# Input projections of a gated three-branch block as two by two block products, seven in place of eight

## The reference

```python
h = _rmsnorm_2(x, norm_g[l])
(u_a, v_a, z_a, c_q, c_kv, k_r, z_b, q_c, k_c, v_c, g_c, z_c, gate_logits) = _split_cols(h @ w_in[l])
y_a = _spatial_gating(u_a, v_a, z_a, ...)
y_b = _mla(c_q, c_kv, k_r, z_b, ...)
y_c = _gla(q_c, k_c, v_c, g_c, z_c, ...)
gates = jax.nn.sigmoid(gate_logits + b_gate[l]).reshape(bn, s, N_BRANCH, d)
merged = (gates[:, :, 0] * (y_a @ w_branch[l, 0]) + gates[:, :, 1] * (y_b @ w_branch[l, 1])
          + gates[:, :, 2] * (y_c @ w_branch[l, 2]))
x = x + merged @ w_out[l]
```

## Time and profile before

| | us |
|---|---|
| median of three runs | 2146.69 (2145.61 to 2146.79) |
| the profiled execution | 2143.29 |
| its span | 2141.5 |
| TensorE busy | 2008.7 (94%) |
| VectorE busy | 902.0 (42%) |
| ScalarE busy | 405.2 (19%) |
| mean granted TensorE clock | 0.976 of full speed |

### The profile page before, as it was taken

How to read it: one execution, slowest core, us unless ns; L and a number is a source line. 1 busy time by engine, 2 the same in 40 slices (tenths; PEclk the granted TensorE clock), 3 DMA queues, 4 the chain that set the end, 5 groups by cost and what they waited for, 6 DMA issues and landing times.

```text
span 2141.5 us, 20633 instructions
## 1 busy us (share of the span) xinstructions
PE 2008.7 (94%) x8153; PEld 908.0 (42%) x8153; DVE 902.0 (42%) x1850; ACT 405.2 (19%) x836; POOL 119.8 (6%) x168
## 2 busy tenths in 40 slices
PE   6999987999999999997899888899999999999998
PEld 2445443333333334454333333333445554445553
DVE  1257555544545445674333323224362432362432
ACT  2146311000000003171100000001222221222220
POOL 1001002000000000000100000000100000100000
PEclk9999987999999999998899999999999999999999
DMA  9267446999999995636799999999533333633331
GB/s 357 91 236 260 173 153 227 427 424 427 426 427 427 428 424 229 246 138 226 282 426 425 426 426 425 425 428 368 192 112 118 118 118 130 221 112 118 118 118 59
DMA packets 95042, 584.23 MB, mean 273 GB/s; under 512 B 10044, under 2 KB 12388, under 8 KB 62044
## 3 DMA queue, kind: packets, MB, share of 16 engines
q1 hardware_dynamic: 84400, 559.96, 64.7%
q0 software_dynamic: 10256, 21.86, 3.2%
q10 hardware_dynamic: 288, 1.05, 0.2%
HBM read 589.05 MB, written 4.26 MB: 277 GB/s over the span
## 4 chain that ended last, share of the span: by engine, by line
PE 80%; DMA 11%; DVE 5%; SPq 2%; ACT 1%; issue 1%; DVEq 0%; POOLq 0%
PE bank L740 25%; PE bank L1042 13%; PE bank L745 6%; DMA ring<-in_w_gate 6%; PE bank L899 5%; PE bank L1056 5%; DMA ring<-in_w_up 4%; PE bank L1120 4%; PE bank L1290 3%; PE bank L967 3%; PE bank L690 2%; PE bank L587 2%; PE bank L678 2%; PE bank L728 1%; DMA ring<-in_w_qkv 1%
## 5 line engine op out<-in xcount | busy, mean ns | idle before, releaser
L740 PE MATMUL bank<-ring,big 128*64 128x512 f32 x2464 | 683.9, 601 | 26.8 <-DMA ring<-in_w_gate 10.2
L740 PEld LDWEIGHTS bank<-ring,big 128*64 128x64 f32 x2464 | 217.8, 138 | 387.4 <-issue 374.4
L1042 PE MATMUL bank<-ring,big 128*128 128x512 f32 (+1 forms) x640 | 282.2, 590 | 0.0
L2051 DVE TENSOR_TENSOR big<-bank,big 128x512 f32<-128x512 f32 x192 | 131.6, 685 | 252.6 <-PE bank L745 251.5
L740 PE MATMUL bank<-big 128*64 128x512 f32 x512 | 227.5, 594 | 0.0
L745 PE MATMUL bank<-big 128*128 128x512 f32 x360 | 180.1, 610 | 0.0
L1042 PEld LDWEIGHTS bank<-ring,big 128*128 128x128 f32 x640 | 117.5, 190 | 126.2 <-issue 126.0
L899 PE MATMUL bank<-ring,big 128*128 128x512 f32 x320 | 141.1, 599 | 3.2 <-ACT big L1334 2.0
L1056 PE MATMUL bank<-ring,big 128*128 128x512 f32 x256 | 111.7, 593 | 0.2
L2255 DVE TENSOR_TENSOR big<-big,bank 128x512 f32<-128x512 f32 x32 | 22.0, 688 | 184.3 <-PE bank L740 184.3
L899 PEld LDWEIGHTS bank<-ring,big 128*128 128x128 f32 x320 | 60.7, 192 | 79.2 <-issue 74.2
(11 more groups left out here) (393 smaller groups left out, 2122.5 us busy)
## 6 DMA issues: line engine op xcount, KB each, us to landing
ring<-in_w_gate SPq DMA_DIRECT2D x52, 2048.0 KB, 18.2
ring<-in_w_up SPq DMA_DIRECT2D x51, 2048.0 KB, 21.7
ring<-in_w_down SPq DMA_DIRECT2D x51, 2048.0 KB, 20.8
ring<-in_w_in SPq DMA_DIRECT2D x26, 2048.0 KB, 7.7
ring<-in_w_ada SPq DMA_DIRECT2D x24, 2048.0 KB, 12.7
big<-in_w_up SPq DMA_DIRECT2D x9, 2048.0 KB, 21.5
big<-in_w_down SPq DMA_DIRECT2D x9, 2048.0 KB, 21.8
big<-in_w_gate SPq DMA_DIRECT2D x8, 2048.0 KB, 19.5
```

The costliest lines, as they stand in the source:

```text
L740: ins = nc.tensor.matmul(bank[half * CAP:(half + 1) * CAP, :], lhs[:, k, half * CAP:(half + 1) * CAP], slot_cols(slots[half], k * step + c ...
L1042: ins = nc.tensor.matmul(u[:, 0:cols], HT2[:, k, tile * P:(tile + 1) * P], w[:, 0:KD * cols].rearrange("p (k n) -> p k n", k=KD)[:, k, :], ...
L2051: return r, V.tensor_tensor(r, bank, GATE[tile // LAT][:, half * 512:(half + 1) * 512], ALU.mult)
```

## The change

The input chunks 6 and 7 become equally wide (472 each). They and the three pairs of gate chunks are computed as a product of two by two blocks: the rows are tile 0 and tile 1, the inner halves are the first and last four blocks of `HT2`, the columns the two chunks. Instead of eight block products of four matmuls, seven are formed: `a11b11`, `a12b21`, `s1t1`, `s2t2`, `s3t3`, `s4b22`, `a22t4`. S1 to S4 are sums of rows, made once a layer by VectorE (`mixed_rows`); T1 to T4 are sums of weights, one 128 by 2048 operation each on VectorE (`mixed_weights`), T2 to T4 written in place of a quarter of the weights in the ring. A product that ends another's sum is accumulated in the same bank (`ADDS_TO`), and VectorE reads the bank in between. The fill list has 144 matmuls a layer, and `POINTS` has smaller numbers in the decay chain. The norm scale, and for gates the bias, is applied afterwards (`gate_rows`; the scaling by ScalarE, `s_paired`). Both chunks of a pair stay in the ring until their last block product, and a load goes to the slot that comes free first (`RELEASED`). Three semaphores are dropped, their waits put on others that rise at the same moment.

```diff
+        after = (LAT + 1) * BRANCHES * D
+        T1 = spare[:, after:after + 2048].rearrange("p (k n) -> p k n", k=4)
+        S12 = cut(2048 + 2 * C_GATE, 1024, 2, 512)
+        S34 = spare[:, after + 2048:after + 3072].rearrange("p (s n) -> p s n", s=2)
+        S1, S2, S3, S4 = (v.rearrange("p (k n) -> p k n", k=4) for v in (S12[:, 0, :], S12[:, 1, :], S34[:, 0, :], S34[:, 1, :]))
+        A11, A12 = HT2[:, 0:4, 0:P], HT2[:, 4:8, 0:P]
+        A21, A22 = HT2[:, 0:4, P:2 * P], HT2[:, 4:8, P:2 * P]
...
-        IN_CHUNKS = [(c, min(512, C_GATE - c)) for c in range(0, C_GATE, 512)]
+        LAST_IN = (C_GATE - 6 * 512) // 2
+        IN_CHUNKS = [(c * 512, 512) for c in range(6)] + [(6 * 512 + i * LAST_IN, LAST_IN) for i in range(2)]
         IN_ORDER = (0, 1, 3, 2, 4, 5, 6, 7)
-        BESIDE = [("in", *IN_CHUNKS[i], tile) for i in IN_ORDER[4:] for tile in range(LAT)]
-        BESIDE_IN = len(BESIDE)
-        BESIDE += [("gate", c, 512, tile) for c in range(2 * BRANCHES) for tile in range(LAT)]
-        BESIDE_GATES = len(BESIDE) - BESIDE_IN
+        HALF = KD // 2
+        PAIRED = [(("in", IN_CHUNKS[6][0]), ("in", IN_CHUNKS[7][0]), LAST_IN)]
+        PAIRED += [(("gate", 2 * n), ("gate", 2 * n + 1), 512) for n in range(BRANCHES)]
+        BESIDE = [("unit", i, tile, KD) for i in (4, 5) for tile in range(LAT)] + [("a11b11", 0, None, HALF)]
+        for g in range(len(PAIRED)):
+            BESIDE += [(name, g, None, HALF) for name in ("a12b21", "s1t1", "s2t2", "s4b22", "s3t3")]
+            if g + 1 < len(PAIRED):
+                BESIDE.append(("a11b11", g + 1, None, HALF))
+            BESIDE.append(("a22t4", g, None, HALF))
+        ADDS_TO = {"s4b22": "s1t1", "s3t3": "s2t2", "a22t4": "s3t3"}
+        T_NUMBER = {"s1t1": 1, "s2t2": 2, "s3t3": 3, "a22t4": 4}
+        STEPS = [(m, k) for m in range(len(BESIDE)) for k in range(BESIDE[m][3])]
+        ENDS = [sum(b[3] for b in BESIDE[:m + 1]) for m in range(len(BESIDE))]
...
-                return (n - second_at) % SLOTS2
+                return min((holder[s] if holder[s] < second_at else second_at + RELEASED.index(stream[holder[s]][0]), s)
+                           for s in range(SLOTS2))[1]
...
-        POINTS = {"rows": (18, 20), "heads": (4, 3), "decay": (4, 6), "logs": (9, 10), "exps": (9, 9),
-                  "turned": (4, 4), "states": (6, 5)}
...
+        POINTS = {"rows": (18, 20), "heads": (4, 3), "decay": (3, 6), "logs": (7, 7), "exps": (7, 6),
+                  "turned": (3, 3), "states": (4, 4)}
...
-                    kind, c, cols, tile = BESIDE[m]
-                    w, at_ = weights((kind, layer, c))
-                    u = BANK_F[n % 2]
-                    if k == 0 and n >= 2:
-                        pe.wait_ge(*beside_taken(n - 2))
-                    ins = nc.tensor.matmul(u[:, 0:cols], HT2[:, k, tile * P:(tile + 1) * P],
-                                           w[:, 0:KD * cols].rearrange("p (k n) -> p k n", k=KD)[:, k, :],
-                                           start=(k == 0), stop=(k == KD - 1))
-                    if k == KD - 1:
+                    name, g, tile, ks = BESIDE[m]
+                    u = BANK_F[F_BANK[n]]
+                    if k == 0 and F_BEHIND[n] is not None:
+                        pe.wait_ge(*beside_taken(F_BEHIND[n]))
+                    if name == "unit":
+                        c, cols = IN_CHUNKS[g]
+                        w, at_ = weights(("in", layer, c))
+                        ins = nc.tensor.matmul(u[:, 0:cols], HT2[:, k, tile * P:(tile + 1) * P],
+                                               w[:, 0:KD * cols].rearrange("p (k n) -> p k n", k=KD)[:, k, :],
+                                               start=(k == 0), stop=(k == ks - 1))
+                        last_use[at_] = (s_fin, n + 1)
+                    else:
+                        x, y = (weights((kind, layer, c)) for kind, c in PAIRED[g][0:2])
+                        b11, b12, b21, b22, cols = quarters(layer, g)
+                        if k == 0 and name in T_NUMBER:
+                            pe.wait_ge(s_mix, 4 * (len(PAIRED) * layer + g) + T_NUMBER[name])
+                        a, b = {"a11b11": (A11, b11), "a12b21": (A12, b21), "s1t1": (S1, T1[:, :, 0:cols]), "s2t2": (S2, b11),
+                                "s4b22": (S4, b22), "s3t3": (S3, b12), "a22t4": (A22, b21)}[name]
+                        ins = nc.tensor.matmul(u[:, 0:cols], a[:, k, :], b[:, k, :], start=(k == 0 and name not in ADDS_TO),
+                                               stop=(k == ks - 1), skip_group_check=True)
+                        last_use[x[1]] = last_use[y[1]] = (s_fin, n + 1)
+                        if name == "a22t4":
+                            last_use[y[1]] = (s_fin, beside_index(layer, "s3t3", g) + 1)
+                    if k == ks - 1:
                         ins.then_inc(s_fin, 1)
-                        last_use[at_] = (s_fin, n + 1)
 
             def in_unit(layer, i, tile):
...
-                pe.wait_ge(s_finA, BESIDE_IN * (layer + 1))
+                pe.wait_ge(s_paired, LAT * (layer + 1))
...
+                    if name == "a11b11":
+                        cols = PAIRED[g][2]
+                        act.wait_ge(s_fin, i + 1)
+                        nc.scalar.activation(pair_rows(g)[1][0], BANK_F[F_BANK[i]][:, 0:cols], ACT.Copy).then_inc(s_finA, 1)
+                    if name == "a12b21" and g == 1:
+                        act.wait_ge(*beside_taken(beside_index(layer, "a22t4", 0)))
+                        for tile in range(LAT):
+                            v = PROJ[:, tile, IN_CHUNKS[6][0]:C_GATE]
+                            nc.scalar.activation(v, v, ACT.Copy, scale=rtot[:, tile:tile + 1]).then_inc(s_paired, 1)
...
+                    (z11, z12), (z21, z22) = pair_rows(g)
+                    u = BANK_F[F_BANK[i]][:, 0:cols]
+                    dve.wait_ge(s_fin, i + 1)
+                    if name == "a12b21":
+                        dve.wait_ge(*beside_taken(beside_index(layer, "a11b11", g)))
+                        V.tensor_tensor(z11, u, z21, ALU.add).then_inc(s_finD, 1)
+                        mixed_weights(layer, g, 2)
+                    if name == "s1t1":
+                        V.tensor_tensor(z22, u, z21, ALU.add).then_inc(s_finD, 1)
+                        mixed_weights(layer, g, 3)
+                    if name == "s2t2":
+                        V.tensor_tensor(z12, u, z21, ALU.add).then_inc(s_finD, 1)
+                        mixed_weights(layer, g, 4)
+                    if name == "s4b22":
+                        dve.wait_ge(*beside_taken(beside_index(layer, "s2t2", g)))
+                        V.tensor_tensor(z12, u, z12, ALU.add).then_inc(s_finD, 1)
+                        gate_rows(layer, g - 1, 0)
+                    if name == "s3t3":
+                        V.tensor_tensor(z22, u, z22, ALU.add).then_inc(s_finD, 1)
+                        gate_rows(layer, g - 1, 1)
+                    if name == "a22t4":
+                        V.tensor_tensor(z21, u, z21, ALU.add).then_inc(s_finD, 1)
+                        mixed_weights(layer, g + 1, 1)
+                        if g + 1 == len(PAIRED):
+                            for tile in range(LAT):
+                                gate_rows(layer, g, tile)
+
+            def gate_rows(layer, g, tile):
+
+                if g < 1:
+                    return
+                dve.wait_ge(*beside_taken(beside_index(layer, "a22t4", g)))
+                v = GS[tile][:, (g - 1) * D:g * D]
+                V.scalar_tensor_tensor(v, v, rtot[:, tile:tile + 1], BG[:, (g - 1) * D:g * D], ALU.mult, ALU.add).then_inc(s_gate, 1)
+
+            def mixed_weights(layer, g, which):
+
+                if g == len(PAIRED):
+                    return
+                b11, b12, b21, b22, cols = quarters(layer, g)
+                t1 = T1[:, :, 0:cols]
+                if which == 1:
+                    for kind, c in PAIRED[g][0:2]:
+                        n = at[kind, layer, c]
+                        dve.wait_ge(w_in[slot_of[n]], 16 * arrival[n])
+                    V.tensor_tensor(t1, b12, b11, ALU.subtract).then_inc(s_mix, one(s_mix))
+                dve.wait_ge(s_mix, so_far(s_mix))
+                if which == 2:
+                    V.tensor_tensor(b11, b22, t1, ALU.subtract).then_inc(s_mix, one(s_mix))
+                if which == 3:
+                    V.tensor_tensor(b12, b22, b12, ALU.subtract).then_inc(s_mix, one(s_mix))
+                if which == 4:
+                    V.tensor_tensor(b21, b21, b11, ALU.subtract).then_inc(s_mix, one(s_mix))
+
...
+            def mixed_rows(layer):
+
+                dve.wait_ge(s_outA, marks["rows_turned", layer][0])
+                V.tensor_tensor(S1, A21, A22, ALU.add).then_inc(s_v, one(s_v))
+                dve.wait_ge(s_v, so_far(s_v))
+                V.tensor_tensor(S2, S1, A11, ALU.subtract).then_inc(s_v, one(s_v))
+                V.tensor_tensor(S3, A11, A21, ALU.subtract)
```

(5 more changed lines are left out.)

108 lines of the change are left out of this document (72 added, 36 removed).

## The result

| | before | with the change |
|---|---|---|
| median, us (four runs each, same chip) | 2146.15 (2143.02 to 2146.79) | 2195.35 (2192.17 to 2200.29) |
| the profiled execution | 2143.29 | 2193.02 |
| its span | 2141.5 | 2191.2 |
| mean granted TensorE clock | 0.976 | 0.964 |

The ratio is 1.0234, with a 95% interval of 1.021 to 1.0259. The forecast was 2138.8 us with a range up to 2149, so the sign was wrong and the time lies 46 us above the range.

A forecast was written before the change was run, and what follows sets the result against it. TensorE, busy 94%, was taken to bound the kernel, VectorE being slack. Per layer 13.7 us saved less 9.7 us of waits gives 4.0, 8 us in all: 2138.8 us, range 2127 to 2149.

The forecast's parts named there:

- the paragraph on transfers: Gate chunk 1's load: VectorE wants it 8.4 us after s3t3, median landing 7.7; nothing taken, up to 1.5 us a layer in range.
- wrong in kind if TensorE waits for a transfer: Stated sign of failure: TensorE waiting for a transfer in the fill, or longer fill records; no size given.
- Taken away: Fill matmuls saved: 3.3 us in the first pair, 10.4 in three gate pairs, 13.7 us a layer if TensorE stays full.
- Weight sum: One 128x2048 sum of weights on VectorE: about 2.3 us, 2.1 with 472 columns; 16 a layer, 36 us.
- the rival of slow sums: Weight sums on ring slots take 3.1 us each; 19 us slower, 2158 us; chance 0.08.
- The walk: New order stepped through with old durations: TensorE waits 9.7 us a layer in the fill, 8 us net gain; chance 0.48.
- (a): Head 7 of tile 0 and next heads: TensorE waits for VectorE's copy of probabilities and late maxima, 1.4 us a layer.
- (b): Head 7 of tile 1: TensorE waits for VectorE's copy behind a weight sum, 1.1 us a layer.
- (c): First tile's decay: TensorE waits 0.3 us behind the first chain and 1.6 behind the cumulative sums, each layer.
- (d): Second tile: TensorE waits for mixed weights 1.8, decay chain 1.1, a bank 1.0 and copies 1.4 us a layer.
- the rival that it was to take in: VectorE's links overlap more: waits some 3 us a layer, 21 us gained, 2125.6 us; chance 0.22.
- The clock: Rival: TensorE's frequent 1 to 2 us gaps lower its clock for eleven steps a layer; 19 us in all, 2158; chance 0.04.

The follow-up runs named there:

- the first experiment: Changed kernel, but each block product's matmuls wait only for the one chunk they read, not both of the pair: 2134.54 us, ratio 0.996 to the kernel before.

## Why the prediction was wrong

**The step that failed** is the paragraph on transfers. It has the event right (gate chunk 1 can load only when `s3t3` of pair 0 has ended) and the landing right (7.7 us, measured 7.7). It then asks when VectorE wants the chunk, finds 8.4 us, and takes nothing. TensorE was never asked. It wants both chunks at the product right behind `s3t3`, 0 us later: six waits, 47.6 us, where the range held 3. The prediction named the sign of it ("wrong in kind if TensorE waits for a transfer") and gave it no chance. It could have been seen: in the third piece of order ahead of the prediction every L1115 row of a block product waits for two slots, also where it reads one chunk alone, as the last rows, of `s2t2`, do. (`a11b11` itself does not stand in that piece.) I read which operand a product uses from the table of operands, and not which semaphores its instruction waits for.

The span grew by 49.7 us. Its account:

| | us | from |
|---|---|---|
| matmuls taken away | -27.4 | sum of the prediction; -26.8 in the fill stretches of the run without sums |
| six waits for a load | +47.6 | waits of TensorE |
| other waits, nearly all for VectorE | +10.4 | 4.6 - 0.4 + 3.3 + 1.5 + 0.7, and 0.7 that the profile puts down to no engine |
| 336 block records of 512 columns last longer | +14 | 123.5 + 45.1, against 110.5 + 44.0 without sums or waits |
| other records of TensorE last longer | +5 | 341.5 against 322.4 us busy in the fill stretches, less the 14 above; 3.1 of it are the three groups of the heads, 44.2 against 41.1 |
| not placed | 0 | less than 1 us |

The two rows of longer records, 19.1 us, hold the clock's part of the loss. The first experiment, without the six waits, has 4.8 us of them, so 14.3 us came with the waits, 2.4 us each.

**What held.** *Taken away*: 13.7 us a layer, shown. *Weight sum*: 2.3 us taken, 2282 ns measured (2118 with 472 columns); the rival of slow sums falls. *VectorE's busy time*: 108 us more forecast, 100.4 measured. *The walk*: it gave 9.7 us a layer, and the first experiment, which has the state that the walk assumed, shows 5.2. By place: (a) 1.4 forecast, 1.19 measured; (b) 1.1 and 1.11; (c) 0.3 and 1.6, measured nothing and 0.77 (L1312); (d) 1.8, 1.1, 1.0 and 1.4, measured 1.66, then 0.67 in layer 1 and nothing in layer 0, where the fill records at the lower clock last as long as the wait would, and the other two not at all. So (a), (b) and the first wait of (d) were good to 0.2 us. In (c) and behind the second tile's decay the walk had the waits too long or where none came; it seems to have carried on delays that VectorE no longer had, which no run tests. (One slip in the recorded range: its lower end, 2127, lies above the 2125.6 us of the rival that it was to take in.)

**The size came out nearly right for a partly wrong reason.** Had the wait been as I read it, the forecast gain of 8 us would have stood against 8.6 to 10.2 by the medians, 12.0 by the fill stretches. But 4.8 us of what was given back are longer records, most of them behind a fall of the clock, which I had at no cost; the waits, at 10.3 against 19.4 us, I had too high. The two errors have opposite signs, and that they nearly cancel is luck.

**The clock** was a rival with 0.04, tied to VectorE's gaps. In the changed kernel it did fall, behind waits of 8 us, which is another cause. Behind VectorE's gaps the first experiment shows 0.91 in one window of 20 us a layer, after the wait of 1.66 us (in layer 1 only behind the next, of 0.67 us), and 1.00 behind those of up to 1.2 us and once that wait was removed. The length of a wait alone does not decide it: with the first product one place later, waits for a load of 3.15 and 2.65 us in layer 0 went with 0.91 and 0.83, and one of 3.21 us in layer 1 with 1.00 throughout. The rule of "TensorE: Matmul & The Clock Gate" in the Trainium skill, section "A second HAM failure mode: psum-queue depth-cycling", which the prediction had cited, is borne out only there and for at most 4.8 us, not for the 19 that I had put on it. Whether the low clock behind the 8 us waits could be avoided while the waits stay was not tried.

**What stays open.** Which waits bring the clock down; the last head's 1.2 us, which moved elsewhere when its cause was taken away; and why the median of the first experiment lies 5 us over its profiled execution, with a spread of 8 us. The untouched first part varies by 5.6 us among the profiled executions, which can be part of it, but only one execution of each kernel was profiled.
